# Two-block transformer step: the second block's attention and branch stages joined into one code block, with four high buffers and sigmoids moved

## The reference, cut to what matters

```python
proj = h @ w_in        # q, k, v of stick-breaking, dilated and GLA attention, GLA's r and a, then 3 x 2048 gate columns
o_sb  = merge_heads(stick_breaking_attention(qa, ka, v_sb))      # 6 heads of 128
o_dil = merge_heads(dilated_mixture(qb, kb, v_dil, slopes))      # 6 heads in 3 groups
o_gla = merge_heads(rms_norm(o_g, gla_out_gain)) * silu(r_gla)   # 4 heads, 128 x 256, decay per key channel
g = sigmoid(gate_cols.reshape(b, t, 3, d))
y = g[:, :, 0] * (o_sb @ w_br_sb) + g[:, :, 1] * (o_dil @ w_br_dil) + g[:, :, 2] * (o_gla @ w_br_gla)
return y @ w_out       # the caller adds gate1 * this to the residual x
```

## Time and profile before

| what | us |
|---|---|
| median of 3 runs (4160.74 to 4171.2) | 4165.59 |
| profiled execution | 4157.45 |
| its span, first to last instruction | 4155.7 |
| TensorE busy in the span | 2378.4 |
| VectorE busy | 2677.0 |
| ScalarE busy | 800.0 |
| stage of the change, 2762.9 to 3268.4 | 505.5 |

### The profile page before, as it was taken

The page is one execution under the profiler, slowest core; times in us unless marked ns, Lnnn a source line. Parts: engine busy times, 40 slices in busy tenths (PEclk is TensorE's granted clock), DMA queues, the critical chain, the costliest instruction groups (busy, mean ns, idle before and its releaser), DMA issues. The chain is left out here.

```text
span 4155.7 us, 28934 instructions
## 1 busy us (share of the span) xinstructions
PE 2378.4 (57%) x10296; PEld 1779.8 (43%) x10296; DVE 2677.0 (64%) x2799; ACT 800.0 (19%) x667; POOL 1203.4 (29%) x605
## 2 busy tenths in 40 slices
PE   7789868860000000000000089998879969999999
PEld 4344437720000000000000078886668758888787
DVE  1877644488888888888888754455675554444444
ACT  1000113300000000000000033323433333333333
POOL 0000000006888888888888500000000000000000
PEclk9899979965555555555555599989999989999999
DMA  5355584488999999999999745533436545555554
GB/s 164 112 192 182 199 312 162 164 303 326 394 379 386 385 403 381 387 383 374 384 377 379 304 153 192 192 126 112 138 110 237 183 147 188 191 192 185 179 192 162
DMA packets 332244, 1029.47 MB, mean 248 GB/s; under 512 B 35256, under 2 KB 35768, under 8 KB 264696
## 3 DMA queue, kind: packets, MB, share of 16 engines
q1 hardware_dynamic: 258424, 491.31, 34.9%
q0 software_dynamic: 73728, 536.90, 32.6%
HBM read 1021.28 MB, written 6.86 MB: 247 GB/s over the span
## 5 line engine op out<-in xcount | busy, mean ns | idle before, releaser
L341 DVE TENSOR_TENSOR slab_low<-ring,slab_high 128x2048 fp32r<-128x2048 f32 x240 | 549.7, 2292 | 716.1 <-ACT slab_high L334 716.1
L536 PE MATMUL bank<-ident,nat 128*128 128x128 f32 x128 | 22.6, 359 | 1497.0 <-DVE nat L517 1457.6
L334 ACT CAST slab_high<-ring 128x2048 fp32r<-128x2048 f32 x304 | 579.5, 1909 | 1052.9 <-PE bank L320 814.1
L1437 DVE SCALAR_TENSOR_TENSOR res<-pool,res 128x2048 f32<-128x2048 f32 x256 | 603.2, 2356 | 101.3 <-DMA pool<-in_peer_v,small 74.7
L536 PEld LDWEIGHTS bank<-ident,nat 128*128 128x128 f32 x128 | 21.7, 193 | 1498.7 <-DVE nat L517 1458.9
L1426 DVE CUSTOM_DVE_ANT_0 pool<-pool,nat 128x2048 f32<-128x2048 f32 x256 | 585.5, 2295 | 96.6 <-DMA pool<-in_peer_u,small 85.7
L318 PE MATMUL bank<-slab_high,left_high 128*128 128x512 f32 x1568 | 616.3, 393 | 34.8 <-DVE slab_low L341 34.8
L319 PE MATMUL bank<-slab_low,left_high 128*128 128x512 f32 x1568 | 614.2, 392 | 0.0
L320 PE MATMUL bank<-slab_high,left_low 128*128 128x512 f32 x1568 | 613.6, 391 | 0.0
L1459 POOL DMA_INDIRECT pool<-in_peer_v,small x256 | 552.3, 2157 | 96.7 <-issue 68.3
L1459 POOL DMA_INDIRECT pool<-in_peer_u,small x256 | 539.8, 2109 | 97.3 <-issue 68.9
(11 more groups left out here) (466 smaller groups left out, 2972.5 us busy)
## 6 DMA issues: line engine op xcount, KB each, us to landing
ring<-in_w_in SPq DMA_DIRECT2D x148, 1024.0 KB, 5.0
ring<-in_w_ada SPq DMA_DIRECT2D x96, 1024.0 KB, 8.6
ring<-in_w_ffn_in SPq DMA_DIRECT2D x88, 1024.0 KB, 5.0
ring<-in_w_ffn_out SPq DMA_DIRECT2D x44, 1024.0 KB, 5.0
ring<-in_w_out SPq DMA_DIRECT2D x32, 1024.0 KB, 5.1
ring<-in_peer_wq SPq DMA_DIRECT2D x16, 1024.0 KB, 5.0
ring<-in_w_br_gla SPq DMA_DIRECT2D x8, 1024.0 KB, 5.0
pool<-modulation SPq DMA_DIRECT2D x5, 1024.0 KB, 6.6
```

Source lines behind the costliest of these rows:

```text
L334: nc.scalar.copy(high[:, n % PARTS], ring[:, g % SLOTS]).then_inc(high_done, 1)
L341: eng.tensor_tensor(dst, ring[:, g % SLOTS], high[:, n % PARTS].bitcast(F32), ALU.subtract)\
L1437: v.scalar_tensor_tensor(res[:, t, :], rows_[r], actv[:, t, bass.ds(i * GB + r, 1)], res[:, t, :], ALU.mult, ALU.add).then_inc(s_free, 1)
```

## The change

- Four high buffers instead of two for the 64 slabs that are low in place: two more lie over `res`. `high_of(g)` picks the buffer by slab number modulo 4. The cast of such a slab waits for the use of the slab four earlier.
- So that `res` is free, SyncE writes it to DRAM at the start of MIX and reads it back at the start of W_OUT2, ahead of that stage's loads.
- `gate_highs` and `gate_lows` run `AHEAD = 2` slabs further at each of their calls. The calls of `gate_loads` and `gate_slabs` are as before.
- `take_gate` copies the banks instead of applying the sigmoid; it stands ahead of the cast of slab 4b+7 instead of 4b+5. The sigmoids are applied on chip in the branch part, one call of 128 x 3072 for each of the four column blocks, on ScalarE.
- The five code blocks are one. Their programs follow each other on each engine without barriers; a few waits replace them. The bodies are otherwise unchanged, and most of the diff is indentation. The core of it:

```diff
+        DEEP = 2 * PARTS
+        def high_of(g):
+            if is_in_place(g):
+                slot = (g - first_slab[GATES]) % DEEP
+                return high[:, slot] if slot < PARTS else over_res[:, slot - PARTS]
+            return high[:, split_index(g) % PARTS]
+        residual_rows = nc.dram_tensor("residual_rows", (P, TT * D), F32, kind="Internal").ap()
...
         def high_part(act, g, i=None):
             if i is not None:
                 act.wait_ge(slabs_used, up + (g - PARTS + 1))
+            elif is_in_place(g) and g - first_slab[GATES] >= DEEP:
+                act.wait_ge(slabs_used, g - DEEP + 1)
+            elif is_in_place(g) and g - first_slab[GATES] >= PARTS:
+                act.wait_ge(s_away, 16)
             elif n >= PARTS:
                 act.wait_ge(slabs_used, split_slabs[n - PARTS] + 1)
-            nc.scalar.copy(high[:, n % PARTS], ring[:, g % SLOTS]).then_inc(high_done, 1)
+            nc.scalar.copy(high_of(g), ring[:, g % SLOTS]).then_inc(high_done, 1)
...
+                sp.dma_start(residual_rows, res_[:, :]).then_inc(s_away, 16)
                 stream(sp, MIX)
...
+        AHEAD, IN_PLACE = DEEP - PARTS, first_slab[W_OUT2] - gate0
         def gate_highs(act, end):
+            end = min(end + AHEAD, IN_PLACE)
             for n in range(at["ACT"], end):
-                if n % 4 == 1 and 0 <= n // 4 - 1 < GATE_BLOCKS:
-                    sigmoid(act, n // 4 - 1)
+                if n % 4 == 3 and 0 <= n // 4 - 1 < GATE_BLOCKS:
+                    take_gate(act, n // 4 - 1)
                 high_part(act, gate0 + n)
...
-                last = nc.scalar.activation(dst, ps[6 + t][:, :], ACT.Sigmoid)
+                last = nc.scalar.copy(dst, ps[6 + t][:, :])
...
         def gate_lows(dve, end):
+            end = min(end + AHEAD, IN_PLACE)
...
+        def stick_on_tensor(pe):
+            for i in range(2):
+                pe.wait_ge(s_hc[i], len(heads) // 4)
...
+                pe.wait_ge(s_ol, min(h + 1, SBH))
...
+        def gla_on_sync(sp):
+            sp.wait_ge(s_do, DHG)
+        def gla_on_gpsimd(g):
+            g.wait_ge(s_mk, 4)
+            g.wait_ge(s_so, SBH)
+            g.wait_ge(s_ds, dk["max"])
...
             gate_loads(sp, 37)
+            sp.wait_ge(s_gs, gm["out"])
             read_back(0)
             read_back(1)
             gate_loads(sp, 44)
+            sp.wait_ge(s_gT2, 4)
             read_back(2)
...
+        def branch_on_scalar(act):
+            gate_highs(act, B0 - 1)
+            for nb in range(OB):
+                if nb < 3:
+                    act.wait_ge(s_back[nb], 16)
+                else:
+                    act.wait_ge(s_gate, GATE_BLOCKS)
+                nc.scalar.activation(sg[nb], sg[nb], ACT.Sigmoid).then_inc(s_sg, 1)
+                gate_highs(act, B0 + 4 * nb + 4)
...
                     sp.dma_start(gate_row, gate_row_src.partition_broadcast(P)).then_inc(s_row_, 16)
+                    if residual_away:
+                        sp.dma_start(res_[:, :], residual_rows).then_inc(s_away, 16)
...
                             dve.wait_ge(s_row_, 16)
+                            if residual_away:
+                                dve.wait_ge(s_away, 32)
```

More of the change, by code:

```diff
@@ new lines, in heads_on_scalar, with copy_pair @@
+        def heads_on_scalar(act):
+            def copy_pair(m):
+                act.wait_ge(s_hT, m + 1)
+                for j in range(2):
+                    _, _, dst, hh, gcol = heads[2 * m + j]
+                    src = ps[m % 4][:, j * T:(j + 1) * T]
+                    if gcol is None:
+                        last = nc.scalar.mul(dst[:, hh, :], src, P ** -0.5 if dst is gqT else 1.0)
+                    else:
+                        last = nc.scalar.mul(dst[:, hh, :], src, gains[:, gcol:gcol + 1])
+                last.then_inc(s_hc[0], 1)
+            gate_highs(act, 2)
+            copy_pair(0)
+            copy_pair(2)
+            gate_highs(act, 5)
+            act.wait_ge(s_hs, hmarks["ss"])
+            nc.scalar.activation(qk_ss, qk_ss, ACT.Sqrt).then_inc(s_hr, 1)
+            for m in (4, 8, 12):
+                gate_highs(act, 7 + (m - 4) // 4)
+                copy_pair(m)
+                copy_pair(m + 2)
+            gate_highs(act, 10)
@@ new lines, in heads_on_tensor @@
+        def heads_on_tensor(pe):
+            for m in range(len(heads) // 2):
+                src = heads[2 * m][0]
+                if m and m % 4 == 0:
+                    gate_slabs(pe, 4 + m // 4)
+                if src is not gla_qk:
+                    pe.wait_ge(s_hn, 1 if src is sb_qk else 2)
+                if m >= 4:
+                    pe.wait_ge(s_hc[m % 2], (m - 4) // 2 + 1)
+                for j in range(4):
+                    src, h, *_ = heads[2 * m + j // 2]
+                    t = j % 2
+                    last = nc.tensor.transpose(ps[m % 4][:, j * P:(j + 1) * P], src[:, t, h * P:(h + 1) * P],
+                                               ident[:, :])
+                last.then_inc(s_hT, 1)
+            gate_slabs(pe, 8)
@@ new lines, in stick_on_scalar @@
+        def stick_on_scalar(act):
+            gate_highs(act, 11)
+            act.wait_ge(s_ss, sm["abs"])
+            nc.scalar.activation(lr, lr, ACT.Exp, scale=-1.0).then_inc(s_sf, 1)
+            act.wait_ge(s_sf, 1)
+            nc.scalar.activation(lr, lr, ACT.Ln, bias=1.0).then_inc(s_sf, 1)
+            gate_highs(act, 13)
+            act.wait_ge(s_ss, sm["logw"])
+            nc.scalar.activation(lb, lb, ACT.Exp).then_inc(s_sf, 1)
+            gate_highs(act, 14)
+            for h in range(SBH):
+                act.wait_ge(s_so, h + 1)
+                nc.scalar.copy(oTh[:, h, :], ps[h][:, 0:T]).then_inc(s_oc, 1)
+            gate_highs(act, 16)
@@ L2253, in _ @@
[L2253 to L2260 removed]
+                heads_on_sync(sp)
+                stick_on_sync(sp)
+                dilated_on_sync(sp)
+                gla_on_sync(sp)
+                branch_on_sync(sp)
+            @block.gpsimd
+            def _(g):
+                stick_on_gpsimd(g)
+                dilated_on_gpsimd(g)
+                gla_on_gpsimd(g)
```

1052 lines of the change are left out of this document (497 added, 555 removed).

## The result

The changed kernel takes a median of 4177.68 us over 20 runs (4167.12 to 4183.79); the kernel before, run beside it, takes 4165.49 us over 20 runs (4154.44 to 4175.11). The ratio is 1.0025 with an interval of 1.0017 to 1.0033: slower by 7 to 14 us, still within 0.3%. The forecast was 4170 us, 4.6 more than before, in a range of 4150 to 4187, with "within 0.3%" as the likeliest outcome. Range and outcome hold, the outcome narrowly, but the shift is more than twice as large as forecast.

The account below looks back on a forecast made before the run. TensorE's waits for low parts (44.9 us) and gate blocks (9.5 us) led in the stage, with TensorE itself the bound in the branches. Shifts of -4.1 + 4.9 + 2.2 + 1.6 = +4.6 us gave 4170 us, range 4150 to 4187.

Parts of the forecast that it names:

- The mechanism: Whole stage: casts two slabs ahead wait for loads landing 5.0 us after release; steps queued behind come 5.0 + 0.1 us later.
- the residual: Residual's way through DRAM around MIX and W_OUT2: taken as 0, bounded by 6 us; rival +6, 4176 us, chance 0.06.
- Slab 4: Heads: starts 3.2 us later, from +4.4 for two low parts, -1.28 table load, +0.1; with the clock's 2.2, +5.4.
- Stick products: End of heads: 1.5 us wait behind slab 10's cast, border's 3.2 and low clock's 2.7 gone; products end +1.0.
- Second stick products, dilated: Sums come +2.1 at the second products, +4.3 with clock; dilated weights +1.6, after slab 20 and border -2.2.
- The start of GLA: VectorE starts at -0.4 behind slab 24's landing; slab 28's cast holds the second level by +3.6, so +3.2.
- Branches: Branch part starts at -4.1; slab 40 adds 4.9 and 2.2 for the clock, slab 44 adds 1.6.
- The clock decides: Rival: waits of 2.7 to 2.9 us at slabs 16, 44 and eight levels lower the clock; +20, 4186 us, chance 0.22.
- Slack wins: Rival: casts behind landings don't hold the attention chains; -38, 4127 us, chance 0.04; half, -19, 4146 us, chance 0.08.
- Only borders and loads: Rival: no reserve reached, only block borders and table loads saved; -11.2 - 3.8, 4151 us, chance 0.06.
- The late sigmoids: Branch part on ScalarE: put-off sigmoids, estimated 2.8 us each, lie between casts two slabs ahead; cost 0.
- The drain that the row didn't show: ScalarE table switches: a rule's 1.38 us drain would make three switches worth 4.1 us more, sum +0.5; not taken.

Follow-up runs that it names:

- no_ahead: The changed kernel with the look-ahead set to 0 and gate blocks taken ahead of the cast of slab 4b+5; 4139.31 us, ratio 0.9939 to before.
- gla_fill_37: no_ahead with casts, low parts and products of slabs 34 and 35, and slab 36 too, moved ahead of the GLA outputs' chain; 4124.98 us, ratio 0.9902.
- take_early: The changed kernel, but from slab 41 on gate blocks are taken ahead of the cast of slab 4b+6; 4170.62 us, ratio 1.0014 to before.
- back_late: The changed kernel with the first two read-backs of gates moved behind the loads of slabs 41 to 46; 4174.85 us, ratio 1.0024 to before.
- after_no_loads: The changed kernel without weight loads for the 44 gate slabs behind the first four, reading a fixed on-chip tensor; 4144.74 us, ratio 0.9951 to before.

## Why the prediction was right and where it was wrong

All shifts are times in after less 8.53 us (the start of the stage) less those in before.

**The mechanism, confirmed.** Casts end their idle time with a DMA, of TensorE's waits for low parts one of 0.7 us is left, levels keep 10.29 us (scaled-key products at 3023.28, 3033.57, 3043.85), slab 40 waits 6.13 us where 6.1 was worked out, the residual costs nothing that shows, and neither MIX nor the rest moved. The four long waits came where they were forecast, 8.14, 13.51, 7.66 and 11.66 us for some 8, 13, 7 to 8 and 11, with granted clocks of 0.81, 0.76, 0.57 and 0.78 in the 6 to 8 us behind them.

**The sum, too low by 9.3 us:** +4.6 against +13.9. 6.5 us of that were missed up to slab 36 (-4.1 against +2.4), 2.8 behind it (+8.7 against +11.5). The prediction gave its own case 5 us either way. The measured median lies 7.7 us above 4170, outside that. It is inside the stated range because this was stretched up to 4187 for the clock case, and that case rested on a boundary that doesn't exist (see the rivals below). That part of the hit is luck.

**Slab 4: right.** It starts +3.0 (+3.2 forecast), slab 5 +4.4 (+5.4). The cost of the clock there was 1.4, not 2.2.

**Stick products: the first miss.** Forecast: a wait of 1.5 us behind the cast of slab 10, short enough for the clock to stay, end +1.0. (The terms as they are written, 5.9 + 1.5 - 3.2 - 2.7, give +1.5, and +4.2 for the start.) Measured: 2.66 us (row above), and a low clock behind it, which the window over the next 7.6 us shows:

```profile
2838.90:2846.50 7.60, 7.59 (x33) 6.56 (x34) 5.26 (x8) 2.81 (x3) 0.00 (x0) 0.78 0.41 160
```

They start +4.7 and end +3.6. Of the 2.7 us that I had booked as the lower clock going, 1.1 came; that is the larger part of the 2.6 us missed here. ScalarE's timeline shows what the head copies stood behind: the cast of slab 10, which had waited 6.06 us for its load.

```profile
2835.49 1.90 ACT L351 CAST residual_parts<-ring 128x2048 fp32r<-128x2048 f32 x1 [6.06 <-DMA ring<-in_w_in]
2837.29 1.56 ACT L1742 ACTIVATE pool<-bank,small 128x256 f32<-128x256 f32 x4
```

**Second stick products, dilated: carried on.** +4.7 instead of +2.1 at the second products, with a wait of 13.51 us (13 forecast), so the step itself was right and only its start was off. The dilated transposes come +5.2, not +1.6: 2.6 of it carried, some 1 added. From slab 19 to the start of GLA, slab 20 and the border gave back 4.8 us (+5.7 to +0.9) of the 5.9 forecast.

**The start of GLA: the second miss.** Forecast: VectorE's chain starts at -0.4, because the low part of one slab, 24, waits for its landing, and then slab 28 holds the second level. Measured: the first level's products come +4.4 and the scaling for the second level on VectorE +8.9 (+3.2 forecast), and there it stays: +7.7 at the eighth level (+1.8 forecast).

The +4.4 is made up of four parts. TensorE comes to this stage at +0.9, not -2.2: that is the earlier misses, carried on. A small load of GLA's gain, which the new wait on SyncE issues later, adds 0.9 with the 0.8 us that TensorE waits for it. Slab 22 then runs at a granted clock of 0.78 and adds 1.4. So the running sums of the decays, which VectorE needs, are ready on TensorE at +3.3. The row of TensorE is the last of them, the window is that of slab 22:

```profile
2992.09 0.39 PE L2210 MATMUL bank<-upto,slab_low_scratch 128*128 128x128 f32 x2
```

```profile
2977.20:2984.20 7.00, 7.00 (x25) 5.65 (x25) 5.71 (x5) 4.76 (x4) 0.00 (x0) 0.78 0.23 89
```

The fourth part is a landing that I left out. ScalarE's timeline, the casts of slabs 24, 25, 26 and 28:

```profile
2973.89 1.90 ACT L351 CAST slab_high<-ring 128x2048 fp32r<-128x2048 f32 x1 [9.23 <-DMA ring<-in_w_in]
2979.41 1.91 ACT L351 CAST slab_high<-ring 128x2048 fp32r<-128x2048 f32 x1 [3.62 <-DMA ring<-in_w_in]
...
2989.47 1.90 ACT L351 CAST residual_parts<-ring 128x2048 fp32r<-128x2048 f32 x1 [4.81 <-DMA ring<-in_w_in]
...
3007.61 1.91 ACT L351 CAST slab_high<-ring 128x2048 fp32r<-128x2048 f32 x1 [8.54 <-DMA ring<-in_w_in]
```

and VectorE's shows who waited for it:

```profile
2991.47 2.29 DVE L358 TENSOR_TENSOR ring_low<-ring,residual_parts 128x2048 fp32r<-128x2048 f32 x1 [4.83 <-ACT residual_parts L351]
2993.68 1.41 DVE L2102 COPY slab_low_scratch<-bank 128x256 f32<-128x256 f32 x4
...
3010.58 1.23 DVE L2115 TENSOR_TENSOR pool<-pool,slab_low_scratch 128x1024 f32<-128x1024 f32 x1 [4.19 <-ACT slab_low_scratch L2179]
```

I had counted two landings in the chain, 24 and 28; that of slab 26 stands there too, 4.83 us on VectorE ahead of the copy with which the levels begin. In before, the low part at this place waited for nothing. But most of the 4.83 us runs beside these sums on TensorE, which end at 2992.48, and the copy starts at 2993.68. So this landing is worth 1.2 us, no more; TensorE's own wait there is 2.66 us against 1.51 before. The step through slab 28 then cost 4.5 us where 3.6 was forecast.

From the last level on, TensorE gave part back, as forecast: its last products, 4.9 us behind the scaled keys before, now follow them at once and come +2.75. That relief of 5 us is as forecast (+1.8 to -3.3 there), but it starts from a larger number. Slab 32, behind a wait of 2.78 us, runs at a granted clock of 0.76 and takes 1.2 us of it back, so the transposes come +3.9, not -3.3, and slab 36 +2.4, not -4.1. (From -3.3, the prediction's 2.0 for the clock and 2.2 back at the border make -3.5; its -4.1 is 0.6 too low by its own terms.)

**Branches: nearly right.** Slab 40's wait is exact, 6.13 us. The clock after it was low as forecast and cost 2.6, not 2.2. Slab 44's wait was 3.55 us, not 2.75, and the clock fell behind it too (0.76 over 3177.0 to 3184.2), 1.6 us that the sum had at nothing. At slab 36 the shift is +2.4, at slab 40 +7.4, at slab 44 +12.4, at the end +13.9.

**Rivals.** "The clock decides" rested on a boundary between a wait of 2.84 and one of 2.86 us. That step is wrong in kind, not in size: no such boundary shows. no_ahead and gla_fill_37 have the same wait at the same place, with one level's slab behind it, and the same instructions up to there (for each a row of TensorE's timeline and the window over the slab; first no_ahead, then gla_fill_37):

```profile
2988.19 0.79 PE L1672 MATMUL bank<-residual_parts,left_high 128*128 128x512 f32 x1 [2.73 <-DVE ring_low L358]
```

```profile
2988.10:2995.40 7.30, 7.21 (x26) 5.85 (x27) 7.09 (x10) 0.59 (x1) 0.00 (x0) 0.78 0.00 1
```

```profile
2986.57 0.50 PE L1672 MATMUL bank<-residual_parts,left_high 128*128 128x512 f32 x1 [2.76 <-DVE ring_low L358]
```

```profile
2986.50:2992.30 5.80, 5.73 (x26) 4.74 (x27) 5.63 (x9) 0.58 (x1) 0.00 (x0) 1.00 0.00 0
```

2.73 us, and the clock fell to 0.78 and cost TensorE 1.5 us; 2.76 us, and it stayed at 1.00. no_ahead_2, which is no_ahead once more, waits 2.76 us there and stays at 1.00 as well:

```profile
2987.50:2993.30 5.80, 5.78 (x26) 4.78 (x27) 5.63 (x8) 0.52 (x1) 0.00 (x0) 1.00 0.01 3
```

The stage doesn't pay for that fall: in no_ahead TensorE then waits 1.32 us for the next slab, in gla_fill_37 2.74. So the added busy time of after, 4.4 us against before and 10.2 against no_ahead, isn't what the clock cost the stage. take_early and back_late have 3.3 and 4.5 us more of it than after and still shorter stages. No run here holds the clock fixed, so its share of the 13.9 us stays open. "Slack wins" is ruled out for this order, and after_no_loads shows why: with a look-ahead of two the stage drops below before's only without landings. "Only borders and loads" was worked out at -15, 3.8 of it for table loads; the joining alone gives -15.9 in the stage without those 3.8, but in the changed kernel the look-ahead swallows it.

**The late sigmoids.** Each of the four took 2.77 us where I had estimated 2.8, and behind slab 44 no slab of TensorE waits at all. One of them, in after's timeline of ScalarE:

```profile
3218.84 2.77 ACT L2297 ACTIVATE pool<-pool 128x3072 f32<-128x3072 f32 x1
```

**The drain that the row didn't show.** In after the first table load among the stick steps is at 2857.09, and its ACTIVATE begins 1.29 us later:

```profile
2857.09 1.28 ACT L1842 ACT_TABLE_LOAD   x1
2858.38 2.13 ACT L1842 ACTIVATE pool<-pool 128x2304 f32<-128x2304 f32 x1
```

The Trainium skill, "ScalarE: Activation LUTs", section "What ACT_TABLE_LOAD costs", counts some 1.38 us of drain beside the load; no row here shows a gap behind one. Slab 4's +3.0 against the +3.2 worked out with 1.28 alone speaks for the row, too.

## What to carry to other kernels

Deeper buffers and a look-ahead are two changes: here the buffers gave some 5 us and the look-ahead in in-order queues took 42. Some 30 of them went because the load ring was no deeper, so that every step written behind an early cast waited for that cast's load. Before moving a step ahead by n places, compare n uses of the consumer with issue, landing and cast, and list every step of another chain that is written behind it, then count each of these places. Count a wait there only as far as it outlasts what the step behind it waits for anyway: one missed landing showed 4.83 us on VectorE and was worth 1.2. And carry the clock along: three of the terms missed here were a clock that fell behind a wait of 2.7 to 3.6 us and was booked at nothing. Where the longest wait lies beside a long chain on one engine, moving just the few slabs whose casts can wait for their loads there without holding anything (9 to 11 us off the stage, gla_fill_37 against the two runs of no_ahead) does what the general look-ahead was to do.

## What the runs showed of the hardware that I had not expected

- **The length of a wait doesn't settle the clock.** Waits of 2.66 (after) and 2.73 us (no_ahead) were followed by 0.78, those of 2.76 us in gla_fill_37 and in the second run of no_ahead by 1.00. What else decides isn't settled by these runs. A fall cost 1.4 to 2.6 us for the slab behind it, and nothing in the stage where the next step was waiting for VectorE anyway.
- **Read-backs double a load's landing.** The two loads issued beside two transfers of 1.5 MB landed after 11.4 and 8.6 us in after, nearly as in before, against 5.0 in the median; moving the read-backs by six loads took 3.4 us off the wait that hung on them.
- **Unchanged code upstream differed** by up to 21 us between profiles, more than the change is worth: a stage that begins and ends with the same instruction has to be compared, not the span.
